# Feed-forward weights of the plain K pairs: two tiles rounded and subtracted as one piece of 2048 columns

## The reference

```python
x = layer_norm(ALPHA * x + merged @ w_out, ...)
ffn = (silu(x @ w_gate) * (x @ w_up)) @ w_down      # w_gate, w_up: 2048 x 5632
x = layer_norm(ALPHA * x + ffn, ...)
```

## Time and profile before

| | before |
|---|---|
| median of 3 runs | 1873.95 us (1873.64 to 1875.46) |
| the profiled execution, its own time | 1874.0 us |
| its span in the trace | 1872.2 us |
| PE busy | 1858.1 us, 99% |
| DVE busy | 1433.3 us, 77% |
| ACT busy | 972.3 us, 52% |
| granted clock of TensorE | 0.998 |

### The profile page before, as it was taken

How to read it: one execution, slowest core, us unless ns; L and a number is a source line. 1 busy time by engine, 2 the same in 40 slices (tenths; PEclk the granted TensorE clock), 3 DMA queues, 4 the chain that set the end, 5 groups by cost and what they waited for, 6 DMA issues and landing times.

```text
span 1872.2 us, 28936 instructions
## 1 busy us (share of the span) xinstructions
PE 1858.1 (99%) x9557; PEld 1532.0 (82%) x9557; DVE 1433.3 (77%) x1947; ACT 972.3 (52%) x1296; POOL 213.5 (11%) x498
## 2 busy tenths in 40 slices
PE   9999999999999999999999999999999999999997
PEld 7888888878888888888888888888888888888886
DVE  7878888897666767676577657799976899856876
ACT  5656566564454545456444436555544555544542
POOL 0202011020023242424000000001000000000000
PEclk9999999999999999999999999999999999999999
DMA  7667667584568676766655676556776566765664
GB/s 274 214 206 229 210 199 237 178 252 159 191 191 248 215 247 215 246 217 199 218 195 186 225 251 196 202 206 226 235 240 196 196 222 217 237 212 180 218 217 149
DMA packets 124414, 400.32 MB, mean 214 GB/s; under 512 B 15312, under 2 KB 28432, under 8 KB 124176
## 3 DMA queue, kind: packets, MB, share of 16 engines
q1 hardware_dynamic: 97904, 351.65, 56.7%
q10 hardware_dynamic: 19200, 28.34, 5.0%
q0 software_dynamic: 7200, 18.88, 3.4%
HBM read 374.15 MB, written 24.66 MB: 213 GB/s over the span
## 4 chain that ended last, share of the span: by engine, by line
PE 97%; DVE 1%; ACT 1%; DMA 0%; issue 0%; SPq 0%; DVEq 0%; ACTq 0%
PE pg L605 75%; PE B L605 21%; DVE gates L1723 1%; DMA raw<-in_weights 0%; ACT whi L1072 0%; PE B L705 0%; ACT hraw L1523 0%; DVE act_b L1715 0%; ACT gates L1510 0%; DVE sm L1723 0%; PE B L853 0%; PE B L925 0%; DVE lnst L2542 0%; ACT vda L1523 0%; DVE lnst L2547 0%
## 5 line engine op out<-in xcount | busy, mean ns | idle before, releaser
L1715 DVE TENSOR_TENSOR wlo<-raw,whi 128x1024 fp32r<-128x1024 f32 (+1 forms) x558 | 666.6, 1198 | 308.2 <-ACT whi L1072 301.0
L1072 ACT ACTIVATE whi<-raw 128x1024 fp32r<-128x1024 f32 (+1 forms) x558 | 578.5, 1040 | 566.1 <-PE pg L605 429.7
L605 PE MATMUL pg<-whi,act_x 128*128 128x512 f32 x2656 | 842.3, 393 | 1.3 <-ACT whi L1072 1.3
L605 PEld LDWEIGHTS pg<-whi,act_x 128*128 128x128 f32 x2656 | 498.5, 188 | 108.4 <-issue 2.2
L605 PE MATMUL pg<-wlo,act_x 128*128 128x512 f32 x1328 | 515.2, 389 | 0.0
L605 PEld LDWEIGHTS pg<-wlo,act_x 128*128 128x128 f32 x1328 | 249.6, 188 | 49.1
L605 PE MATMUL pg<-whi,act_a 128*128 128x512 f32 x812 | 260.0, 390 | 0.0
L605 PEld LDWEIGHTS pg<-whi,act_a 128*128 128x128 f32 x812 | 152.4, 188 | 32.1 <-DVE act_a L1715 0.2
L605 PE MATMUL pg<-whi,act_b 128*128 128x512 f32 x512 | 158.5, 389 | 0.0
L605 PE MATMUL pg<-wlo,act_a 128*128 128x512 f32 x406 | 158.0, 389 | 0.0
L605 PE MATMUL B<-whi,act_a 128*128 128x512 f32 x460 | 149.8, 389 | 0.0
(11 more groups left out here) (335 smaller groups left out, 1908.1 us busy)
## 6 DMA issues: line engine op xcount, KB each, us to landing
raw<-in_weights SPq DMA_DIRECT2D x564, 512.0 KB, 4.2
raw_b<-in_weights SPq DMA_DIRECT2D x82, 512.0 KB, 4.2
turn_q<-hraw POOLq DMA_DIRECT2D x10, 512.0 KB, 6.3
hraw<-turn_q POOLq DMA_DIRECT2D x40, 128.0 KB, 4.9
turn_c<-hraw ACTq DMA_DIRECT2D x8, 512.0 KB, 3.4
qT<-turn_c ACTq DMA_DIRECT2D x32, 128.0 KB, 4.7
turn_q<-hraw ACTq DMA_DIRECT2D x6, 512.0 KB, 3.8
gates<-turn_q ACTq DMA_DIRECT2D x24, 128.0 KB, 4.8
```

Of the source, the lines that this page charges most:

```text
L605: return nc.tensor.matmul(o, l, r, start=start, stop=stop)
L1072: return nc.scalar.activation(o, i, ACT.Copy, scale=scale)
L1715: return V.tensor_tensor(o, a, b, op)
```

## The change

For groups 1 to 10, plain tiles from s = 4 on, that is tiles 6 and 7, 10 and 11, 14 and 15 of each group, are split in pairs: one ACTIVATE and one TENSOR_TENSOR of 2048 columns over two neighbouring slots in place of two of each over 1024 columns. The first two K pairs (tiles 0 to 3), the mixed tiles and the down products stay as they are.

```diff
+        def is_paired(f, s):
+
+            return 4 <= s < 2 * TPG and s // 2 not in spos(f)
...
+            def pair_item(m):
+
+                landed_in(act, m)
+                landed_in(act, m + 1)
+                act.wait_ge(tile_used, m + 1 - AHEAD)
+                copy(whi[:, m % RING:m % RING + 2], raw_pair(m)).then_inc(hi_done, 2)
...
                     if f and is_mixed(f, s + AHEAD) and (s + AHEAD) % 2:
                         mixed_item(f, n, s + AHEAD)
+                    elif f and is_paired(f, s + AHEAD):
+                        if s % 2 == 0:
+                            pair_item(n + s + AHEAD - 1)
                     elif f or s > TPG:
                         split(n, s)
...
+            def pair_item(m):
+
+                r = m % RING
+                dve.wait_ge(hi_done, m + 2)
+                dve.wait_ge(tile_used, m + 1 - AHEAD)
+                tt(wlo[:, r:r + 2], raw_pair(m), whi[:, r:r + 2], ALU.subtract).then_inc(lo_done, 2)
...
                     if f and is_mixed(f, s + AHEAD):
                         mixed_item(f, n, s + AHEAD)
+                    elif f and is_paired(f, s + AHEAD):
+                        if s % 2 == 0:
+                            pair_item(n + s + AHEAD - 1)
                     else:
                         split(n, s)
```

## The result

| | before | after |
|---|---|---|
| median of 9 runs | 1873.97 us | 1880.75 us (1879.82 to 1881.27) |
| span of the profiled execution | 1872.2 us | 1879.0 us |

A forecast was written before the change was run, and what follows sets the result against it. TensorE, with no idle time, was taken to bound the kernel, so helper savings are worth nothing. Five stalls of 1.18 us, 5.9 in all, added to 1874.0 gave 1879.9 us; range 1876.0 to 1886.5.

The forecast's parts named there:

- The price of the pieces: On VectorE a 2048-column subtraction takes 2290 ns; on ScalarE a 2048-column rounding takes 1.92 us, with 1.80 as low end.
- The pair's window: From the first matmul of tile 4, group 8: pair usable at 4.65 us, tile 6 due at 4.85, 0.20 to spare.
- The sentence on the Trainium skill: The page says each instruction pays a fixed cost, one large piece only once; on VectorE 0.06 us a pair.
- the pair of step 4: In heavy groups, with VectorE's product ahead: tile 6 can begin at 3.46 us, due at 3.64, so it just fits.
- The delay: Pair of tiles 14 and 15 pushes transposition, ScalarE's rounding, q1 copy and VectorE's shared additions; additions 1.68 us later.
- The stall and the groups: TensorE waits at tile 5 of groups 2, 3, 4, 7 and 8, 1.18 us each, 5.9 us in all.
- the restart: After a stall on TensorE, five matmuls take 1.39 us in place of 1.30, adding 0.08 to each stall.
- The last hidden block: In the last down product: 1.22 us of idle time before it, could come 0.46 later, taken as hidden.
- Rival 1: No change in time, 1874 to 1877 us: cheaper wide roundings, or ScalarE's fixed order not holding q1; chance 0.18.
- Rival 2: Every pair late, its 0.20 margin gone, and five stalls longer by 0.2: 1883 to 1887 us; chance 0.15.
- rival 3: Raw buffers come back too late, a pair waits for a landing: 1 to 3 us more, about 1882; chance 0.04.
- Rival 4: The change doesn't pair what it says, or the order is another, so splits stay: 1874 us; chance 0.03.

The follow-up runs named there:

- the three kernels without the stalls: Changed kernel with transposition ahead of step 12's subtraction, 1874.26 us; tiles 14, 15 split singly in groups 1, 2, 3, 6, 7, 1875.05; in all groups, 1874.26.
- the last experiment: Kernel pairing only tiles 6, 7, 10, 11, with an extra VectorE subtraction of 16 or 256 columns ahead of each pair's subtraction: 1878.34 and 1883.23 us.
- that link cut: Changed kernel with ScalarE rounding the transposed block behind the copy of q1 instead of ahead of it: 1876.97 us against 1874.31, ratio 1.0016.
- the window runs: Kernel pairing only tiles 6, 7, 10, 11, plus a 16- or 256-column subtraction between rounding and pair's subtraction: ratios 1.0021 and 1.0045 to the kernel before.

## Why the prediction was right, point by point

**What bounds the kernel.** Right: what VectorE and ScalarE save bought no time, since TensorE had none idle in that stretch. None of the three kernels without the stalls, with 30, 25 and 20 pairs, can be told from the kernel before.

**The price of the pieces.** 2290 and 1920 ns were taken, 2291 and 1915 measured. The low end from the rounding of 1152 columns was wrong; the straight line through two widths of the same operation held. The sentence on the Trainium skill ("VectorE: DVE Perf Modes", the errata on SBUF-source operations) held in both halves: the trace agrees with its 2291 ns, and one large piece did pay the fixed cost once, which lowered VectorE's busy time and not the kernel's.

**The pair's window.** Right that it fits, too high in the margin: 0.11 and not 0.20. Of the 0.09 between them, 0.06 lies in the 0.03 for VectorE to start. Its wide subtraction starts 0.09 after the rounding ends (1577.89 + 1.92 = 1579.81, then 1579.90), although the short piece in the last experiment starts 0.03 after it (1214.60 + 1.92 = 1216.52 and 1216.55). In the kernel where VectorE's piece alone is wide it is 0.08, in the one where ScalarE's alone is wide 0.03, so it goes with the width of VectorE's piece. Why stays open. A further 0.02 is ScalarE's start, 0.28 behind tile 4 in group 1 (1214.60 against 1214.32 in the last experiment) in place of 0.26. In the heavy groups the pair of step 4 fitted as well: no tile 6 of the changed kernel is longer by more than 0.04.

**The delay.** 1.68 forecast, 1.71 measured, by the steps named: transposition, ScalarE's rounding, q1, additions. In the list of what would show it the text said that the first addition would come 7.4 us after the rounding; its own working gives 1579.56 - 1572.46 = 7.10, and 7.13 was measured. The 7.4 was a slip.

**The stall and the groups.** 1.18 forecast, 1.22 measured, in the five groups named and in no other; in all 6.1 us against 5.9. The difference is the 0.03 of the delay and 0.01 of rounding: the restart, given as 0.08, is 1.39 - 1.30 = 0.09 by the prediction's own figures. The other 0.7 of the 6.8 us lie outside the stalls, and most of them are no effect of the change, as shown above. The last hidden block, taken as hidden, was hidden: its subtraction comes 7.12 later (1811.86 in place of 1804.74) where TensorE is 6.76 later, and TensorE doesn't stop there.

One deadline was missed. The first tile of the last down product writes banks that the shared additions of group 10 read, and waits for the last of these (`down_ready`, the count `shared_free`). VectorE and TensorE there, in the kernel before:

```profile
1791.70 1.29 DVE L1715 TENSOR_TENSOR alt_b<-B,alt_b 128x512 f32<-128x512 f32 x2
```
```profile
1794.88 0.39 PE L605 MATMUL B<-whi,act_x 128*128 128x512 f32 x1
```

and after:

```profile
1800.12 1.29 DVE L1729 TENSOR_TENSOR alt_b<-B,alt_b 128x512 f32<-128x512 f32 x2
```
```profile
1801.55 0.43 PE L609 MATMUL B<-whi,act_x 128*128 128x512 f32 x1
```

The last addition ended at 1791.70 + 1.29 = 1792.99, 1.89 ahead of the tile, and now ends at 1800.12 + 1.29 = 1801.41, 0.14 ahead: no margin is left, and that tile is 0.08 longer. The prediction looked only at the hidden block in this place. With a delay of 2.24, in the kernel with two subtractions more, the same tile is 0.58 longer.

**The releaser.** The text expected the waits to be put down to VectorE. For the changed kernel the view names ScalarE in all five; the ends of the instructions settle it, as shown above.

**The rivals.** Rival 1 had two conditions. Cheaper wide roundings fell with the 1915 ns. It also named ScalarE's order as the doubtful link and gave, without it, a delay of 1.01, a stall of 0.51 and 2.6 us in all. With that link cut the runs show 1.06, 0.55 and 2.7 us, and with it 1.71 and 1.22: the link is real. Rival 2 (every pair late) fell with the run that pairs two thirds, though the window runs show that little more than 0.1 us would have made it true for them. Nothing of rival 3 was seen: no wait of TensorE is ended by a load, and the window runs lose what their extra piece explains. Rival 4 fell with the 30 pieces of 2048 columns on each engine.

In one execution of the kernel with the transposition first, a pair's subtraction in group 8 started 0.45 after its rounding had ended, in place of 0.09, with no wait that the profile shows, and tile 6 was 0.32 longer. Rounding and subtraction, then tile 6:

```profile
1594.25 2.87 ACT L1076 ACTIVATE whi<-raw 128x2048 fp32r<-128x2048 f32 x2 [1.44 <-PE B L609]
```
```profile
1596.62 2.29 DVE L1729 TENSOR_TENSOR wlo<-raw,whi 128x2048 fp32r<-128x2048 f32 x1 [0.83 <-issue]
```
```profile
1599.06 0.47 PE L609 MATMUL B<-whi,act_a 128*128 128x512 f32 x1
```

The first of the two roundings ends at 1594.25 + 1.92 = 1596.17. In the kernel before, the rest of tile 6 starts at 1593.93 and takes 1.22, so it is there 3.08 ahead of the tile, and such a slip would have cost nothing. That is a second price of a pair, seen once in that kernel's 30 pairs; the cause of the slip is open.

## What to carry to other kernels

When the bounding engine has no idle time, a saving on its helpers is worth nothing, and each edit there is to be read as a change of deadlines: find the smallest margin between the end of a helper's work and its use, and follow every queue behind the edited instruction to it, on both helpers and across the turn from one to the other. Joining two pieces into one makes the first piece as late as the second; what stands behind the joined piece in a fixed order pays too, and here the price was paid in the next group. Work that is ready anyway should stand ahead of a long wait, not behind it.

## What was not expected of the hardware

The 0.15 us from the end of what TensorE waits for to its matmul was read before the change; the runs add that it stays the same whether the tile is 0.1 or 1.5 us late. The first matmul after a stall is followed by the next one 0.30 to 0.31 us later in place of 0.23, at both; so even the smallest miss of tile 6, 0.1 us, costs 0.08 on top. One wait was shorter: behind the last shared addition, with two subtractions more, the first matmul of the last down product starts 0.10 after its end (1802.44 + 1.29 = 1803.73, then 1803.83). A wide subtraction of 2048 columns starts 0.09 us after the rounding it waits for, a narrow one 0.03.
